# Gate and value groups of the four feed-forward up projections take their weight chunks in turn

## The reference: two transformer blocks in fp32

```python
# first block
gu = h @ w_ffn_in[l]                       # 2048 x (2*5632)
g_ffn, u_ffn = jnp.split(gu, 2, axis=-1)
y = (jax.nn.silu(g_ffn) * u_ffn) @ w_ffn_out[l]
# second block
u = h @ w_up                               # 2048 x (2*5632)
u_pad = jnp.pad(u, ((0, 0), (2, 0), (0, 0)))
y = conv_b
for i in range(3):
    y = y + conv_w[i] * u_pad[:, i:i + S]
gate, val = jnp.split(y, 2, axis=-1)
return (jax.nn.silu(gate) * val) @ w_down
```

## Time and profile before

| what | value |
|---|---|
| time, median of 2 runs | 2692.68 us (2692.58 to 2692.77) |
| time of the profiled execution | 2690.75 us |
| its span | 2688.9 us |
| PE busy | 2571.8 us, 96% of the span |
| DVE busy | 1835.1 us, 68% |
| ACT busy | 1317.3 us, 49% |
| POOL busy | 31.0 us, 1% |
| mean granted PE clock | 0.976 of full |
| DMA | 550.69 MB, mean 205 GB/s |

### The profile page before, as it was taken

The page is one execution under the profiler, slowest core; times in us unless marked ns, Lnnn a source line. Parts: engine busy times, 40 slices in busy tenths (PEclk is TensorE's granted clock), DMA queues, the critical chain, the costliest instruction groups (busy, mean ns, idle before and its releaser), DMA issues.

```text
span 2688.9 us, 41837 instructions
## 1 busy us (share of the span) xinstructions
PE 2571.8 (96%) x14922; PEld 2231.3 (83%) x14922; DVE 1835.1 (68%) x2243; ACT 1317.3 (49%) x1701; POOL 31.0 (1%) x36
## 2 busy tenths in 40 slices
PE   5899989999997999999999989999999999999997
PEld 4778878888786888888888868888888888888886
DVE  6879997777787555677555565566677774477764
ACT  1445555666444444434444445555555554455542
POOL 0000000000000000000000000030000000000000
PEclk8699999999998999999999999999999999999999
DMA  9899984555593666798666655544555566655564
GB/s 373 314 303 308 315 275 134 165 157 156 188 300 123 185 184 185 229 305 268 185 186 187 188 157 177 176 145 152 174 180 185 184 187 196 186 175 185 186 202 133
DMA packets 491943, 550.69 MB, mean 205 GB/s; under 512 B 18776, under 2 KB 448864, under 8 KB 491840
## 3 DMA queue, kind: packets, MB, share of 16 engines
q1 hardware_dynamic: 489840, 542.10, 63.3%
q0 software_dynamic: 2000, 7.22, 0.9%
HBM read 547.14 MB, written 2.11 MB: 204 GB/s over the span
## 4 chain that ended last, share of the span: by engine, by line
PE 81%; DVE 9%; issue 4%; ACT 4%; DMA 1%; SPq 1%; DVEq 0%; ACTq 0%; POOL 0%
PE psg L1829 76%; PE pss L1829 4%; DVE w_lo L1170 2%; ACT w_hi L659 1%; DVE gate_acc_mix L1151 1%; DVE first_acc L1248 1%; DMA raw<-in_w_in 1%; SPq L523 1%; DMA stage<-in_w_ada 1%; DVE Pq L1378 0%; ACT X L740 0%; DVE proj L1134 0%; ACT sq L740 0%; DVE decay L1380 0%; DVE decay L1366 0%
## 5 line engine op out<-in xcount | busy, mean ns | idle before, releaser
L1829 PE MATMUL psg<-X,w_hi 128*128 128x512 f32 x4512 | 1605.1, 401 | 28.1 <-issue 14.8
L1170 DVE TENSOR_TENSOR w_lo<-raw,w_hi 128x1024 fp32r<-128x1024 f32 x832 | 1009.8, 1229 | 655.6 <-ACT w_hi L659 646.5
L659 ACT ACTIVATE w_hi<-raw 128x1024 fp32r<-128x1024 f32 x832 | 867.5, 1056 | 857.6 <-PE psg L1829 808.2
L1829 PE MATMUL psg<-X,w_lo 128*128 128x256 f32 x4512 | 1248.9, 282 | 0.0
L1829 PEld LDWEIGHTS psg<-X,w_hi 128*128 128x128 f32 x4512 | 846.8, 189 | 226.7 <-issue 18.8
L1829 PEld LDWEIGHTS psg<-X,w_lo 128*128 128x128 f32 x4512 | 858.7, 190 | 13.8 <-issue 1.4
L1829 PE MATMUL psg<-hid,w_hi 128*128 128x512 f32 x1664 | 581.4, 394 | 0.2 <-issue 0.2
L1829 PE MATMUL psg<-hid,w_lo 128*128 128x256 f32 x1664 | 458.1, 279 | 0.0
L1829 PEld LDWEIGHTS psg<-hid,w_hi 128*128 128x128 f32 x1664 | 309.4, 187 | 71.6 <-issue 0.6
L1829 PEld LDWEIGHTS psg<-hid,w_lo 128*128 128x128 f32 x1664 | 312.0, 187 | 3.6
L644 ACT ACTIVATE half<-psg 128x512 f32<-128x512 f32 x205 | 119.3, 582 | 10.3 <-PE psg L1829 10.1
(11 more groups left out here) (301 smaller groups left out, 1551.4 us busy)
## 6 DMA issues: line engine op xcount, KB each, us to landing
raw<-in_w_in SPq DMA_DIRECT2D x212, 512.0 KB, 4.5
raw<-in_w_ffn_in SPq DMA_DIRECT2D x176, 512.0 KB, 3.8
raw<-in_w_up SPq DMA_DIRECT2D x176, 512.0 KB, 5.1
raw<-in_w_ffn_out SPq DMA_DIRECT2D x88, 512.0 KB, 4.7
raw<-in_w_down SPq DMA_DIRECT2D x88, 512.0 KB, 3.5
gate_w_mix<-in_w_ada SPq DMA_DIRECT2D x160, 256.0 KB, 5.5
stage<-in_w_ada SPq DMA_DIRECT2D x64, 512.0 KB, 10.7
raw<-in_w_out SPq DMA_DIRECT2D x64, 512.0 KB, 4.4
```

What stands on the lines that cost most here:

```text
L659: nc.scalar.activation(w_hi[:, half_slot(j, p), :, :], raw[:, slot_of(j, p), :, :], ACT.Copy).then_inc(hi_ready, 1)
L1170: nc.vector.tensor_tensor(w_lo[:, hs, :, :], raw[:, slot_of(j, p), :, :], w_hi[:, hs, :, :].bitcast(F32), ALU.subtract).then_inc(raw_used, 1)
L1829: return nc.tensor.matmul(out_, l, r_, start=start, stop=stop)
```

## The change

A new argument `by_k` of `Job` sorts the list of turns by K quarter first and by group second, and the four up projections set it. Turns 0, 2, 4, 6 are then the gate group's quarters 0 to 3 and turns 1, 3, 5, 7 the value group's. The gate group ends in turn 6 and the value group in turn 7; the value group begins in turn 1. The same list orders the loads on SP, the splits on ACT and DVE and the matmuls on PE. `chunks_done`, on which `take_half` waits, counts by the new place of the end. No instruction is added or taken away; waits and their targets move with the turns.

```diff
-    def __init__(self, name, iters, groups, ada=(), korder=None):
+    def __init__(self, name, iters, groups, ada=(), korder=None, by_k=False):
...
-        self.offs = [sum(self.chunks[:n]) for n in range(len(groups))]
         self.n = sum(self.chunks)
         self.where = [(g, c) for g in range(len(groups)) for c in range(self.chunks[g])]
-        self.ends = {self.offs[g] + self.chunks[g] - 1: g for g in range(len(groups))}
+        if by_k:
+            self.where.sort(key=lambda gc: (gc[1], gc[0]))
+        self.ends = {p: g for p, (g, c) in enumerate(self.where) if c == self.chunks[g] - 1}
+        self.done = {g: p + 1 for p, g in self.ends.items()}
...
-            Job("up1a", 12, [wide(w_ffn_in, 0, DT, 0, CW), wide(w_ffn_in, 0, DT, HID, CW)]),
+            Job("up1a", 12, [wide(w_ffn_in, 0, DT, 0, CW), wide(w_ffn_in, 0, DT, HID, CW)], by_k=True),
...
-            Job("up1b", 10, [wide(w_ffn_in, 0, DT, 12 * CW, CW), wide(w_ffn_in, 0, DT, HID + 12 * CW, CW)]),
+            Job("up1b", 10, [wide(w_ffn_in, 0, DT, 12 * CW, CW), wide(w_ffn_in, 0, DT, HID + 12 * CW, CW)], by_k=True),
...
-            Job("up2a", 12, [wide(w_up, 0, DT, 0, CW), wide(w_up, 0, DT, HID, CW)]),
+            Job("up2a", 12, [wide(w_up, 0, DT, 0, CW), wide(w_up, 0, DT, HID, CW)], by_k=True),
...
-            Job("up2b", 10, [wide(w_up, 0, DT, 12 * CW, CW), wide(w_up, 0, DT, HID + 12 * CW, CW)]),
+            Job("up2b", 10, [wide(w_up, 0, DT, 12 * CW, CW), wide(w_up, 0, DT, HID + 12 * CW, CW)], by_k=True),
...
         def chunks_done(j, i, g):
 
-            return j.h0 + i * j.n + j.offs[g] + j.chunks[g]
+            return j.h0 + i * j.n + j.done[g]
```

## The result

The changed kernel takes 2858.28 us (median of 2 runs, 2856.89 to 2859.67) against 2692.68 us: ratio 1.0616, 95% interval 1.0599 to 1.0633. The forecast was 2853 us. The profiled execution of the changed kernel took 2856.89 us with a span of 2855.0 us, 166.1 us over the span before.

The account below looks back on a forecast made before the run. PE's main matmuls were taken as the bound (76% of the chain). Terms 22 + 0.9 + 96.6 + 8 - 2.8 + 36 = 160.7 us on 2690.75 give 2851.5; the median stands 1.9 higher: 2853 us, range 2810 to 2880.

Parts of the forecast that it names:

- The bank waits: Up projections: one turn instead of four before a bank pair's next use, so PE waits in turns 0 and 1.
- SwiGLU layer: up1a, up1b: PE waits 1.1 us an iteration with restart, 20 passages, 22 us, plus 0.9 at job ends.
- Convolution layer: up2a, up2b: value group's sum behind the gate function costs 4.83 us an iteration, 96.6 us over 20 passages, before clock loss.
- The clock: up2a, up2b: PE's idle of some 4.1 us drops the granted clock each iteration, 1.8 us each, 36 us.
- Job ends: Down projections: turn 0 waits for banks, 0.9 us after SwiGLU jobs; with late w_lo in turn 4, 8 us after convolution jobs.
- First iteration of up2a: PE's 2.74 us wait for w_lo of turn 4 goes, as the gate group ends in turn 6: -2.8 us.
- The held clock: Rival: clock holds in the convolution layer despite the 4.1 us wait, 36 us go, 2817 us; chance 0.22.
- The clock stayed at 1.00 in the SwiGLU layer: Rival judged: clock falls in up1a and up1b too, 36 us more, 2889 us; chance 0.05.
- Late weights: Rival: the 1 us margin for w_lo at turn 4 goes, 20 us more, 2873 us; chance 0.05.

Follow-up runs that it names:

- experiment 4: Changed kernel, but the gate group's function runs on ACT and DVE after the value group's copy and sum in turn 7; 2792.07 us, 1.0378 of the kernel before.
- experiment 6: Kernel before with by_k on up2a and up2b alone, half before w_hi and sum before w_lo where a group ends; 2787.36 us, ratio 1.0355.
- experiment 7: Kernel before with by_k on up2a and up2b alone, the gate group's convolution without its last tap; 2805.49 us, ratio 1.0424.
- experiment 5: Kernel before with by_k on up1a and up1b alone, half before w_hi and sum before w_lo where a group ends; 2693.2 us, ratio 1.0007.
- defer_gate: Same run as experiment 4: changed kernel, gate group's function moved behind the value group's copy and sum; 2792.07 us, 1.0378 of the kernel before.
- early_conv: Same run as experiment 6: by_k on up2a and up2b alone, halves and sums first where a group ends; 2787.36 us, 1.0355 of the kernel before.
- fill_gap: Changed kernel plus 16 unused matmuls on PE after turn 0 of each iteration of up2a and up2b; 2822.91 us, 1.049 of the kernel before.
- early_swiglu: Same run as experiment 5: by_k on up1a and up1b alone, halves and sums first where a group ends; 2693.2 us, 1.0007 of the kernel before.
- self_once: Kernel before, old order, PE waiting for its own last chunk in turn 4 of each up projection's first iteration only; 2691.48 us, ratio 0.9999.

## Why the prediction was right

- **The bank waits.** In up2a ACT's `w_hi` of turn 6 starts at 2122.13 and the next at 2129.37, 7.24 us on (predicted 7.21); the value group's sum ends at 2131.58 + 0.68 = 2132.26, 10.13 on (10.13):

```profile
2122.13 1.06 ACT L661 ACTIVATE w_hi<-raw 128x1024 fp32r<-128x1024 f32 x1 [1.72 <-PE psg L1831]
...
2128.83 0.63 ACT L960 ACTIVATE csg<-cacc 128x512 f32<-128x512 f32 x1 [1.70 <-DVE cacc L1801]
2129.37 1.04 ACT L661 ACTIVATE w_hi<-raw 128x1024 fp32r<-128x1024 f32 x1
2130.31 0.58 ACT L646 ACTIVATE half<-psg 128x512 f32<-128x512 f32 x1
```

and on DVE:

```profile
2131.58 0.68 DVE L1136 TENSOR_TENSOR cu<-psg,half 128x512 f32<-128x512 f32 x1
```

In up1a the same lengths are 969.25 - 965.76 = 3.49 (3.49) for the copy and 971.47 + 0.68 - 965.76 = 6.39 (6.41) for the sum. PE starts at 2132.40, 0.14 us after the sum; the prediction took 0.04, read after a `w_lo`. In the convolution layer experiments 4, 6 and 7 each took one piece out of this chain, and the wait of turn 1 shrank by about that piece; experiment 5 did so in the SwiGLU layer.
- **SwiGLU layer.** 21.7 us against 22.9. An iteration is 23.46 to 23.78 us, predicted 23.7. With turns of 2.83 us a passage costs 23.78 - 22.60 = 1.18 us, a little over the 1.1 of the prediction; where the iteration is 23.46 the turns take 2.77 us, a gain that was not forecast.
- **Convolution layer.** 135.5 us against 130.7. The wait was put at 4.1 us; 19 of the 20 are 4.10 to 4.16, the first is 4.03. The 4.8 us more come from the clock and from the first iteration, below.
- **The clock.** 1.8 us an iteration was taken from between 0 and 2.5; it is 2.1, some 5 us more in all. That the drop is the rule, since 4.1 is nearer to 4.52 than to 2.74, held. But it was partly luck, for the row that kept the clock through 2.74 us is no safe bound. From one such wait to the next `defer_gate` has 20 stretches in up2a and up2b: 17 read 0.94, behind waits of 2.25 to 2.67 us, and three read 1.00, behind waits of 1.90, 2.29 and 2.30. In `early_conv`, with waits of 2.71 to 2.95 us, 17 of 20 read 0.89 to 0.95. So the length of the wait alone did not decide.
- **Job ends.** The wait for `w_lo` in turn 4 of dn2a and dn2b is 2.73 us, not 3.5. The step was right and its lengths were those of the loop; the last iteration is written outside the loop and its chain is shorter. There ACT's copies of turns 6, 7 and 0 start at 2298.81, 2305.75 and 2313.55, 6.94 and 7.80 us apart, where the loop has 7.24 (above) and 8.24 (2100.69 to 2108.93), together 0.74 us less. Why it is shorter there is open.
- **First iteration of up2a.** This term was wrong. Its 2.74 us wait for `w_lo` is gone, as forecast, but the prediction counted -2.8 us and left out the wait for out2's banks (1.69 us, above). From the first matmul of up2a to the second iteration's first it was 1953.70 - 1926.87 = 26.83 us and is 1977.79 - 1951.26 = 26.53, so 0.3 us were won. The last 0.34 of the 26.53 are the wait of turn 0, which the prediction counts with the passages; even without it the gain is under 0.7. The two waits for `w_lo` that are left in PE's list, 5.5 us in all, stand in the down projections:

```profile
2316.00 0.47 PE L1831 MATMUL psg<-hid,w_hi 128*128 128x512 f32 x1 [2.73 <-DVE w_lo L1172]
...
2740.03 0.47 PE L1831 MATMUL psg<-hid,w_hi 128*128 128x512 f32 x1 [2.74 <-DVE w_lo L1172]
```

- **The rivals.** The held clock (2817) is what `fill_gap` shows artificially at 2823, with 7 us of filling in it. The clock stayed at 1.00 in the SwiGLU layer. The Trainium skill (TensorE: Matmul & The Clock Gate, section "A second HAM failure mode: psum-queue depth-cycling") has a kernel whose clock went down and up again through micro-idles between groups of matmuls. The trace does not agree for the pauses of 0.3 to 0.4 us in up1a, at 1.00; the clock falls in up2a, with pauses of 4.1 us. Late weights did not occur in the loops of the changed kernel; in `defer_gate`, where the bank waits are short, they are the next limit.
- **The sum.** The profiled time rose by 166.1 us where 160.7 were forecast. Its misses go both ways and cancel in part, which is luck: 4.8 us too few in the convolution layer and 2.7 in stages that the change doesn't touch, against 1.2 too many in the SwiGLU layer and 0.9 at the job ends.

None of the variants beats the kernel before; `early_swiglu` equals it. No run has the new order in the convolution layer without any wait, so that the order itself costs nothing is shown for the SwiGLU layer alone. Four bank pairs for these jobs were not tried; after experiment 4, I would expect them to meet the weight slots next in the convolution layer.

## What to carry to other kernels

Double-buffered PSUM banks are only worth the turns that lie between a group's end and the next use of its banks: here four turns (11.3 us) became one (2.8 us), against a copy and a sum out of the banks that take 2.9 us by themselves and 10.1 us behind the neighbour's function. Ask it too of the first iteration, where the banks belong to the job before. Before groups are interleaved, add up the in-order work on each engine that empties them, from the end of a group to the release of its banks, and put the release first. Here a wait of 4.1 us on TensorE in each iteration cost nearly half as much again in granted clock (2.1 us on the 4.83 of the passage).

## What was not expected of the hardware

At clock 1.00 a turn of 16 matmuls in up1a takes one of two lengths, 2.77 or 2.83 us; in dn1a it is 2.80. With no restart in the loop it is 2.83 from the second iteration on (kernel before and `early_swiglu`), after a restart it may be either, and the shorter one ends again at a group's end without a restart (`self_once`). ACT's first copies, each started by the end of a turn, show it in the changed kernel, 2.77 apart:

```profile
954.67 1.06 ACT L661 ACTIVATE w_hi<-raw 128x1024 fp32r<-128x1024 f32 x1 [1.71 <-PE psg L1831]
957.44 1.06 ACT L661 ACTIVATE w_hi<-raw 128x1024 fp32r<-128x1024 f32 x1 [1.71 <-PE psg L1831]
960.21 1.06 ACT L661 ACTIVATE w_hi<-raw 128x1024 fp32r<-128x1024 f32 x1 [1.71 <-PE psg L1831]
```

In all this moves some 0.4 us an iteration of eight turns. What sets it is open.
